# Gate tables from one 256-column product per token, with their sum shared by ScalarE and VectorE

## What is computed

```python
s_val, s_idx = lax.top_k(s, PEER_TOPK)
cand = s_val[..., 0, :, None] + s_val[..., 1, None, :]
best, pos = lax.top_k(cand.reshape(...), PEER_TOPK)
gate = jax.nn.softmax(best, -1)
...
    ub = jnp.take(u_emb, eb, axis=0)
    vb = jnp.take(v_emb, eb, axis=0)
    act = jax.nn.gelu(jnp.einsum('td,ted->te', tb, ub), approximate=False) * gb
    return jnp.einsum('te,ted->td', act, vb)
```

## Time and profile before

| | us |
|---|---|
| median of 3 runs | 3558.95 |
| lowest, highest | 3555.56, 3562.87 |
| the profiled execution | 3554.96 |
| its span | 3553.3 |
| PE busy in the span | 3459.0 (97%) |
| DVE busy | 2150.5 (61%) |
| POOL busy | 1952.3 (55%) |
| ACT busy | 1108.4 (31%) |
| mean granted clock of PE (1 is full) | 0.992 |

### The profile page before, as it was taken

The page is one execution under the profiler, slowest core; times in us unless marked ns, Lnnn a source line. Parts: engine busy times, 40 slices in busy tenths (PEclk is TensorE's granted clock), DMA queues, the critical chain, the costliest instruction groups (busy, mean ns, idle before and its releaser), DMA issues.

```text
span 3553.3 us, 45903 instructions
## 1 busy us (share of the span) xinstructions
PE 3459.0 (97%) x17471; PEld 2986.3 (84%) x17471; DVE 2150.5 (61%) x3761; ACT 1108.4 (31%) x1245; POOL 1952.3 (55%) x938
## 2 busy tenths in 40 slices
PE   6899999999999999999999999999999999999998
PEld 2588888775788889999999999999888888888886
DVE  1546665114514468982776876773576777767666
ACT  3322211133323223223333434343322323332333
POOL 0344432212444346776556565657777777777764
PEclk9999999999999999999999999999999999999999
DMA  9556642238544226777677677768988888988872
GB/s 368 193 189 202 215 153 91 81 131 312 206 148 148 94 86 250 270 281 277 234 287 278 240 290 290 280 256 343 356 329 325 328 320 321 333 323 313 324 287 96
DMA packets 292279, 874.73 MB, mean 246 GB/s; under 512 B 17913, under 2 KB 78665, under 8 KB 238272
## 3 DMA queue, kind: packets, MB, share of 16 engines
q1 hardware_dynamic: 227888, 525.37, 42.5%
q0 software_dynamic: 38688, 281.15, 19.5%
q10 hardware_dynamic: 25584, 66.69, 5.0%
HBM read 803.78 MB, written 69.32 MB: 246 GB/s over the span
## 4 chain that ended last, share of the span: by engine, by line
PE 88%; DVE 5%; DMA 5%; issue 1%; ACT 1%; POOL 0%; ACTq 0%; DVEq 0%; SPq 0%
PE bank L1928 80%; DMA ring<-in_w_mod 3%; PE bank L2262 2%; DMA neurons<-tiny 2%; PE bank L2145 2%; PE bank L2117 1%; PE bank L1936 1%; DVE low L1346 1%; PE bank L2245 0%; PE bank L2070 0%; DVE hT_lo L1341 0%; DVE acc L1823 0%; DVE b L1711 0%; PE bank L2209 0%; DVE tiny L1706 0%
## 5 line engine op out<-in xcount | busy, mean ns | idle before, releaser
L753 POOL TENSOR_TENSOR split<-ring,split 128x1024 fp32r<-128x1024 f32 x544 | 1305.3, 2412 | 628.9 <-ACT split L1056 627.2
L1928 PE MATMUL bank<-h_hi,split 128*128 128x384 f32 (+1 forms) x4608 | 1226.6, 343 | 4.8 <-POOL split L753 3.7
L1056 ACT ACTIVATE split<-ring 128x1024 fp32r<-128x1024 f32 x544 | 577.2, 1062 | 1560.0 <-PE bank L1928 1548.0
L1928 PE MATMUL bank<-split,a_split 128*128 128x512 f32 x4608 | 1045.0, 389 | 0.1
L1928 PEld LDWEIGHTS bank<-split,a_split 128*128 128x128 f32 x4608 | 865.0, 188 | 179.8 <-POOL split L753 0.5
L1928 PEld LDWEIGHTS bank<-h_hi,split 128*128 128x128 f32 x4608 | 839.6, 188 | 25.5 <-POOL split L753 4.6
L1928 PE MATMUL bank<-h_lo,split 128*128 128x384 f32 (+1 forms) x2304 | 785.3, 341 | 0.0
L1928 PEld LDWEIGHTS bank<-h_lo,split 128*128 128x128 f32 x2304 | 434.1, 188 | 9.4
L448 POOL TENSOR_TENSOR ring_lo<-ring,w_hi 128x2048 fp32r<-128x2048 f32 x47 | 219.5, 4670 | 394.6 <-ACT w_hi L441 394.6
L1814 DVE TENSOR_TENSOR acc<-acc,bank 128x512 f32<-128x512 f32 x372 | 251.5, 683 | 289.8 <-PE bank L1928 288.9
L1928 PE MATMUL bank<-hT_hi,w_hi 128*128 128x512 f32 (+1 forms) x768 | 288.4, 376 | 11.9 <-POOL ring_lo L669 4.6
(11 more groups left out here) (287 smaller groups left out, 3638.0 us busy)
## 6 DMA issues: line engine op xcount, KB each, us to landing
ring<-in_u_emb SPq DMA_DIRECT2D x128, 1024.0 KB, 4.8
ring<-in_v_emb SPq DMA_DIRECT2D x128, 1024.0 KB, 5.2
ring<-in_w_mod SPq DMA_DIRECT2D x64, 1024.0 KB, 9.7
ring<-in_w_in SPq DMA_DIRECT2D x48, 1024.0 KB, 5.1
ring<-in_w_mod SPq DMA_DIRECT2D x64, 512.0 KB, 4.6
neurons<-tiny ACTq DMA_DIRECT2D x128, 192.0 KB, 2.7
gate_table<-b ACTq DMA_DIRECT2D x6, 4096.0 KB, 14.7
weigh<-neurons SPq DMA_DIRECT2D x32, 768.0 KB, 8.8
```

The costliest lines, as they stand in the source:

```text
L753: nc.gpsimd.tensor_tensor(split[:, r % 2, 1, at].bitcast(F32R), ring[:, r % 4, :, :].rearrange("p k n -> p (k n)")[:, at], split[:, r % 2, ...
L1056: nc.scalar.activation(split[:, q % 2, 0, at].bitcast(F32R), ring[:, q, :, :].rearrange("p k n -> p (k n)")[:, at], ACT.Copy)\
L1928: last = mm(out_, left[a].bitcast(F32R), right[b].bitcast(F32R), start=start and n == 0, stop=stop and n == 2)
```

## The change

Everything in it concerns the gate table, the dots and where their operands lie.

- **PE**: the matrix of ones is now that of the second key and is the one that is loaded as weights. The two gate matrices (of the first key) stand side by side as 256 columns. So each token has one product of 256 columns in place of two of 128. The high and the low part of its table come out side by side, not added. A group fills banks 6 and 7.
- **ACT** copies the high parts (128 columns of every 256) to `stage` and counts `gate_staged`.
- **DVE** then adds the low parts onto `stage` and counts `gbank_free`. This addition for group g stands in DVE's order behind the `onehots` of group g + 1; that of a chunk's last group stands behind the dot of its last unit.
- **DVE, onehots**: per token one comparison as before, and one operation of 128 x 256 in place of two of 128 x 128.
- **Operands of the dots**: bank 7 is no longer free for `iota`. It goes to the last 128 columns of bank 3. `h2` keeps 1920 columns in the banks, and its last 128 go to SBUF, in `h2_last`. So each of the 128 dots is done in two pieces, 1920 columns against the banks and 128 columns with both inputs in SBUF; the second piece's sums go to `nval_last`, and one addition joins them after the last dot.

```diff
             def copy_h2():
                 act.wait_ge(score_copied, 4)
-                nc.scalar.activation(bank[:, 0:4, :], h2_sparse.rearrange("p (b n) -> p b n", b=4), ACT.Copy)\
-                   .then_inc(h2s_made, 1)
+                nc.scalar.activation(bank_rows[:, D - P:D], iota, ACT.Copy).then_inc(h2s_made, 1)
+                nc.scalar.activation(bank_rows[:, 0:D - P], h2_sparse[:, 0:D - P], ACT.Copy).then_inc(h2s_made, 1)
+                nc.scalar.activation(h2_last, h2_sparse[:, D - P:D], ACT.Copy).then_inc(h2s_made, 1)
...
             def stage_group(count, at):
                 act.wait_ge(onehot_used, count)
-                nc.scalar.activation(stage[:, :, at:at + 4].rearrange("p i t -> p t i"),
-                                     bank[:, 6, :].rearrange("p (t i) -> p t i", t=4), ACT.Copy)\
-                    .then_inc(gbank_free, 1)
+                parts = bank[:, 6:8, :].rearrange("p b (t h i) -> p (b t) h i", h=2, i=P)
+                nc.scalar.activation(stage[:, :, at:at + 4].rearrange("p i t -> p t i"), parts[:, :, 0, :], ACT.Copy)\
+                    .then_inc(gate_staged, 1)
...
                 if k == 3:
-                    act.wait_ge(rows_used, SLOTS)
+                    act.wait_ge(nval_summed, 1)
                     nc.scalar.activation(nval, nval, ACT.Gelu).then_inc(nval_gelu, 1)
...
                 if n == 0:
-                    dve.wait_ge(h2s_made, 1)
-                rows = gathered_rows[n % 3].rearrange("p (b n) -> p b n", b=4)
-                nc.vector.tensor_tensor_reduce(out=rows, in0=sparse_bank, in1=rows, scale=1.0, scalar=0.0,
-                                               op0=ALU.mult, op1=ALU.add, accum_out=nval[:, n:n + 1])\
-                    .then_inc(rows_used, 1)
+                    dve.wait_ge(h2s_made, 3)
+                for at, h2_rows, sums in ((slice(0, D - P), bank_rows[:, 0:D - P], nval),
+                                          (slice(D - P, D), h2_last, nval_last)):
+                    rows = gathered_rows[n % 3][:, at]
+                    last = nc.vector.tensor_tensor_reduce(out=rows, in0=h2_rows, in1=rows, scale=1.0, scalar=0.0,
+                                                          op0=ALU.mult, op1=ALU.add, accum_out=sums[:, n:n + 1])
+                last.then_inc(rows_used, 1)
...
-                    nc.vector.tensor_scalar(onehot[:, grp % 2, s, 0, :].bitcast(F32R), iota_bank, expT[:, 0, tok],
+                    nc.vector.tensor_scalar(onehot[:, grp % 2, s, 0, :].bitcast(F32R), iota_bank, expT[:, 1, tok],
                                             None, ALU.is_equal)
-                    for part, gates in enumerate((gate_hi, gate_lo)):
-                        last = nc.vector.tensor_scalar(onehot[:, grp % 2, s, 1 + part, :].bitcast(F32R), iota_bank,
-                                                       expT[:, 1, tok], gates[:, tok], ALU.is_equal, ALU.mult)
+                    last = nc.vector.scalar_tensor_tensor(
+                        onehot[:, grp % 2, s, 1:3, :].bitcast(F32R), iota_bank.unsqueeze(1).to_broadcast([P, 2, P]),
+                        expT[:, 0, tok], gate_parts_at[:, :, tok].to_broadcast([P, 2, P]), ALU.is_equal, ALU.mult)
                 last.then_inc(onehot_made, 1)
...
+            def stage_group(grp):
+                at = 4 * (grp % 16)
+                dve.wait_ge(gate_staged, grp + 1)
+                place = stage[:, :, at:at + 4].rearrange("p i t -> p t i")
+                parts = bank[:, 6:8, :].rearrange("p b (t h i) -> p (b t) h i", h=2, i=P)
+                nc.vector.tensor_tensor(place, place, parts[:, :, 1, :], ALU.add).then_inc(gbank_free, 1)
...
                     onehots(group)
+                    if group % 16:
+                        stage_group(group - 1)
                     group += 1
                 dot(unit - 3)
+                if (unit - PRE) % CHUNK_UNITS == CHUNK_UNITS - 1:
+                    stage_group(group - 1)
...
                 for s in range(4):
-                    for part in range(2):
-                        last = mm(bank[:, 6, s * NK:(s + 1) * NK], onehot[:, buf, s, 1 + part, :].bitcast(F32R),
-                                  onehot[:, buf, s, 0, :].bitcast(F32R), start=part == 0, stop=part == 1)
+                    last = mm(bank[:, 6 + s // 2, (s % 2) * 2 * NK:(s % 2 + 1) * 2 * NK],
+                              onehot[:, buf, s, 0, :].bitcast(F32R),
+                              onehot[:, buf, s, 1:3, :].rearrange("p h n -> p (h n)").bitcast(F32R),
+                              start=True, stop=True)
                 last.then_inc(onehot_used, 1)
```

17 lines of the change are left out of this document (12 added, 5 removed).

## The result

The changed kernel takes **3621.5 us** (median of four runs, 3619.5 to 3625.9) against 3558.5 before: ratio 1.018, 95% interval 1.016 to 1.0195. The forecast was 3544. The time lies inside the stated range (3518 to 3640), but on the other side of no change. What happened is, nearly to the place, the rival "caught behind POOL" (3618).

What follows compares the result with a forecast made beforehand. PE was taken to bound the gate stage, with DVE near the edge. Cheaper products -35.5, PE's waits for DVE's longer chain +18.7, the search +1.5: -15 us, giving 3544, range 3518 to 3640.

Steps and rivals of the forecast that it cites:

- caught behind POOL: Rival, gate stage: DVE's second dot piece is held until POOL's split ends; 3618 us in all, chance 0.30.
- The bound: Gate stage: PE limits, busy 115.31 of 116 us in a chunk; DVE is near the edge with 79.6 us.
- the wrong side: Gate stage: the second dot piece starts after POOL's split and is held, from an addition of about 1.36 us on.
- The products: PE, gate groups: four products of 256 columns replace eight, saving 0.37 us a group, 35.5 us over 96 groups.
- the addition's time: DVE, gate stage: adding the low parts onto `stage` takes 1.2 us, between bounds 0.68 and 1.67.
- the threshold: DVE, gate stage: the addition's length, about 1.36 us, from which the second dot piece falls behind POOL's split; margin 0.16.
- The comparisons: DVE, gate stage: the next group's `onehots` take 0.67 us a token, 2.68 us a group.
- Being caught: Gate stage: PE goes on at T0 + 12.65, 3.26 us late at 24 places and about 2.4 at six; 93 us.
- The chunk's start: ACT at a chunk's end waits for DVE's last addition before issuing the table's store; cost nothing.
- The clock: PE, if the piece is held: waits let its clock fall, 1.2 us lost at least, 30 times, up to 3700.
- Pieces in the search: Search, 1341 to 1445 us: some 11 two-piece dots delay POOL's splits; 1.5 us lost (0 to 6).

Runs made afterwards that it cites:

- e3: The changed kernel without DVE's addition, the low parts left out of the gate tables; 3525.3 us, ratio 0.9895.
- e2: The changed kernel with DVE's addition on 512 adjacent words instead of words 64 apart, so the tables are wrong; 3530.5 us, ratio 0.9924.
- e5: The changed kernel with DVE's addition covering three of a group's four tokens (384 columns in place of 512); 3544.7 us, ratio 0.9972.
- e1: The changed kernel with the second dot piece reading its token operand from the banks, not from h2_last; 3561.5 us, ratio 1.0006.
- e9: e7 with half of each gate table stored at the chunk's end (2 MB in place of 4 MB); 3523.2 us, ratio 0.9899.
- e7: The changed kernel with each gate-stage dot behind the next group's comparisons and addition, its short piece first; 3538.5 us, ratio 0.9945.
- e6: The kernel before with only the dots made in two pieces, gate products unchanged and no addition on DVE; 3558.7 us, ratio 1.0011.

## Why the prediction was wrong, step by step

- **The bound** (PE, with DVE near the edge) was right, and so was the reading of the wrong side: being caught by the split, from an addition of 1.36 us on.
- **The products**: 0.37 a group forecast, 0.43 measured (5.07 to 4.64, and 9.23 to 8.80 in a unit of one group). 41.3 us gained instead of 35.5; e3 bears it out.
- **The step that failed is the addition's time.** Taken were 1.2 us, between bounds 0.68 and 1.67; measured 1.34 in the mean, 1.37 in the unit above. ACT's copy was the wrong guide: its surcharge of 0.49 is for one side at the distance of 64 words, and DVE's addition reads and writes at it; its surcharge is 0.66 (e2). (The Trainium skill, SBUF — State Buffer, "Specifications (TRN2)", wants two or more accesses in each line of 16 bytes for full bandwidth. DVE's 1.34 against 0.68 in e2 agrees with it; it gives no size.) That moved the second piece from 0.16 us ahead of the split to 0.06 behind it: 0.17 by the addition, 0.05 because the split came earlier. The prediction named the threshold, 1.36, and then gave the side beyond it 0.30 against 0.40, on a margin of 0.16 us with an uncertainty of 0.5. With an estimate that coarse the two sides were an even bet, and their prices weren't: e5 shows 77 us between them. Which side came true was decided by very little: since the 19 pieces started 0.03 to 0.07 behind the split, an addition some 0.07 us shorter would have been enough to escape (an estimate from these distances; between 1.05 and 1.34 us no length was run).
- **The comparisons**: 2.68 us a group forecast, 2.60 measured (2024.57 to 2027.17).
- **Being caught**: 3.26 us a place forecast, 3.33 measured; piece until the split's end, PE at T0 + 12.65 forecast, T0 + 12.63 measured. (The rule of the Trainium skill, SBUF — State Buffer, "Who interferes with whom", held for the pieces shown, with 2.50 us against 0.29 in e1, where one input lies in the banks.) But there were 19 such waits and not 24 and six of 2.4: after unit 7 (counted from 0) there was only one, of 0.76 us, since that unit began 3.33 late and, in five chunks of six, ran partly at the lower clock, which gave ACT and DVE time; and in chunks 2 to 6 the wait at the chunk's second group took the place of the one behind its first unit.
- **The chunk's start** was costed at nothing, for the store's issue. That was the wrong question: not when the store goes out counts, but that ACT's first copy comes 3.3 us late by its length. Before, the weight loads stood idle 1.0 there; with an addition of 1.3 between that copy and PE, and PE 0.43 earlier, it is 2.95. With the slow stretches: 5 x 1.95 + 5 x 1.5 = 17 us. e9 takes away the whole of these waits and stretches, 22.2 us from e7. The earlier trace rows had those five waits for ACT's copy; they were read as a small number and not as places without reserve.
- **The clock**: the fall was named, at 1.2 us or more each for 30 places, and left out of the 3618; measured are 21 of 1.5, 31 us in all.
- **Pieces in the search**: 1.5 us forecast (0 to 6). The stage starts 3.0 later in the profiled executions, but 2.3 of that arise ahead of the first dot, for a reason that stays open; 0.7 is left for the pieces. The medians differ by 1.6 (e6), hardly clear of noise.
- That the rival's total came so near (3618 against 3621.5) is in part luck. Errors cancelled in it: fewer and shorter waits (-19 us, 73.8 in place of 92.6) and cheaper products (-6) against the clock (+31) that its 3618 left out.
